# Four later modulation rounds of a two-block network: loaded over ScalarE's queue into the buffer of x and multiplied inside the first layer's attention

## The reference

```python
silu_c = jax.nn.silu(c)
silu_cc = jax.nn.silu(c_ctx)
for l in range(DEPTH):                               # DEPTH = 2
    mod = silu_c @ mod_w[l] + mod_b[l]
    mod_c = silu_cc @ mod_w[l] + mod_b[l]
    x, xc = trunk_layer(x, xc, mod, mod_c, ...)

# in trunk_layer
shift, scale, gate = jnp.split(mod[:, None, :], 3, axis=-1)
z = split_columns((rmsnorm(x, pre_g) * (1 + scale) + shift) @ w_in)
y_mla, yc_mla = mla_branch(...)                      # attention, 8 heads
y_pool = pool_branch(z, pool_w, pool_scale)
y_gla, yc_gla = gla_branch(...)                      # gated linear attention
out = merge_branches(z, y_mla, y_pool, y_gla, w_branch_mla, w_branch_pool, w_branch_gla, w_out)
x = x + gate * rmsnorm(out, post_g)
```

## Time and profile before

| what | value |
|---|---|
| median of 3 runs | 1536.61 us (1534.15 to 1538.3) |
| the profiled execution, its own time | 1537.87 us |
| its span in the profile | 1535.7 us |
| mean granted TensorE clock | 0.954 of full speed |
| PE busy | 1368.0 us, 89% of the span |
| ACT, DVE, POOL busy | 42%, 56%, 48% |
| DMA | 180.79 MB, 118 GB/s on average |

### The profile page before, as it was taken

How to read it: one execution, slowest core, us unless ns; L and a number is a source line. 1 busy time by engine, 2 the same in 40 slices (tenths; PEclk the granted TensorE clock), 3 DMA queues, 4 the chain that set the end, 5 groups by cost and what they waited for, 6 DMA issues and landing times.

```text
span 1535.7 us, 24492 instructions
## 1 busy us (share of the span) xinstructions
PE 1368.0 (89%) x10240; PEld 1147.7 (75%) x10240; DVE 864.3 (56%) x1237; ACT 638.4 (42%) x1004; POOL 733.3 (48%) x512
## 2 busy tenths in 40 slices
PE   5798899999999999688899899878799888799997
PEld 1654688777776788374888799868688777799996
DVE  2567514441423441756587468579898635588812
ACT  3545322433332324446334564747421123555542
POOL 0520054323223544050696658738644205499994
PEclk9899999999999999799999999979899999899998
DMA  8320033344334433030334335525222133355652
GB/s 333 130 69 14 29 96 96 110 153 163 112 133 181 137 97 98 27 122 15 123 122 133 104 124 153 164 83 178 70 85 70 56 97 118 90 188 181 183 186 86
DMA packets 49118, 180.79 MB, mean 118 GB/s; under 512 B 5488, under 2 KB 6512, under 8 KB 48624
## 3 DMA queue, kind: packets, MB, share of 16 engines
q1 hardware_dynamic: 48864, 177.13, 35.4%
q10 hardware_dynamic: 144, 2.10, 0.3%
HBM read 178.16 MB, written 1.05 MB: 117 GB/s over the span
## 4 chain that ended last, share of the span: by engine, by line
PE 67%; DVE 18%; ACT 5%; DMA 4%; issue 3%; POOL 2%; SPq 0%; ACTq 0%; DVEq 0%
PE ps L368 17%; PE ps L372 17%; PE ps L369 16%; PE ps L370 16%; DMA panels<-weights 3%; DVE work L1844 2%; POOL panels_r L412 1%; ACT panels_hi L402 1%; PE ps L965 1%; POOL panels_r L413 1%; DVE work L1286 1%; DMA const_sb<-constants 1%; DVE work_r L1289 1%; DVE small L1013 1%; DVE work L808 1%
## 5 line engine op out<-in xcount | busy, mean ns | idle before, releaser
L412 POOL TENSOR_TENSOR panels_r<-panels,panels_hi 128x512 fp32r<-128x512 f32 x254 | 373.0, 1468 | 782.2 <-ACT panels_hi L402 780.7
L369 PE MATMUL ps<-h_sb_r,panels_hi 128*128 128x256 f32 (+1 forms) x1408 | 452.9, 322 | 0.0
L402 ACT ACTIVATE panels_hi<-panels 128x1024 fp32r<-128x1024 f32 x254 | 267.6, 1057 | 407.9 <-PE ps L370 235.9
L413 POOL TENSOR_TENSOR panels_r<-panels,panels_hi 128x512 fp32r<-128x512 f32 x254 | 374.2, 1473 | 0.0
L368 PE MATMUL ps<-hi_sb_r,panels_hi 128*128 128x512 f32 (+1 forms) x784 | 278.1, 355 | 27.8 <-DVE h_sb_r L683 14.0
L369 PEld LDWEIGHTS ps<-h_sb_r,panels_hi 128*128 128x128 f32 x1408 | 276.0, 196 | 17.7 <-issue 0.7
L370 PE MATMUL ps<-hi_sb_r,panels_r 128*128 128x512 f32 (+1 forms) x784 | 272.1, 347 | 0.0
L368 PE MATMUL ps<-h_sb_r,panels_hi 128*128 128x256 f32 x624 | 184.1, 295 | 12.2 <-DVE h_sb_r L664 7.6
L368 PEld LDWEIGHTS ps<-hi_sb_r,panels_hi 128*128 128x128 f32 x784 | 152.4, 194 | 53.6 <-DVE h_sb_r L683 15.3
L368 PE MATMUL ps<-work_r,panels_hi 128*128 128x256 f32 (+1 forms) x560 | 177.0, 316 | 13.6 <-POOL panels_r L413 9.4
L370 PE MATMUL ps<-h_sb_r,panels_r 128*128 128x256 f32 x624 | 180.0, 288 | 0.0
(11 more groups left out here) (326 smaller groups left out, 1881.8 us busy)
## 6 DMA issues: line engine op xcount, KB each, us to landing
panels<-weights SPq DMA_DIRECT2D x328, 512.0 KB, 3.6
x_sb<-x_in SPq DMA_DIRECT2D x1, 2048.0 KB, 8.0
x_sb<-x_in ACTq DMA_DIRECT2D x1, 2048.0 KB, 10.7
const_sb<-constants SPq DMA_DIRECT2D x1, 1216.0 KB, 10.5
out<-x_sb SPq DMA_DIRECT2D x2, 512.0 KB, 3.1
vec_sb<-vectors SPq DMA_DIRECT2D x1, 725.0 KB, 11.8
small<-c_in SPq DMA_DIRECT2D x1, 8.0 KB, 1.8
```

What stands on the lines that cost most here:

```text
L369: pe.matmul(o, lhsT.hi, rhs.lo, start=False, stop=False)
L402: act.activation(panels_hi[:, m:m + PANEL * P], panels[:, n:n + PANEL * P], ACT.Copy).then_inc(panel_rounded, 1)
L412: pool.tensor_tensor(panels_r[:, at:at + half], panels[:, at:at + half], panels_hi[:, m:m + half], ALU.subtract)
L413: pool.tensor_tensor(panels_r[:, at + half:at + 2 * half], panels[:, at + half:at + 2 * half], panels_hi[:, m + half:m + 2 * half], ALU.su ...
```

## The change

The later rounds leave the merge and the ring. Their panels go to the end of the stream (`MOD_LATER`), SP no longer loads them, and ACT's queue loads them in 16 parts of 1 MB (two panels) into the two halves of `x_sb`. A part is a quarter of a round, 8 products. Part n is multiplied in step n+1 of the first layer's attention: parts 0, 4, 8 and 12 at the end of the step, the others between the scores and the transposes. The rounds are summed in bank 7, and so the values of attention, which used banks 6 and 7 in turn, use the two halves of bank 6 (in both layers, with a wait for `gated` that asks for one pair more).

```diff
+MOD_LATER = ((0, 2), (1, 0), (1, 1), (1, 2))
+MOD_PARTS = 4
+        lent_loaded, lent_used = [sem(f"mod_part_loaded{b}") for b in range(2)], sem("mod_part_used")
+        def load_mod_part(act, n):
+            if n >= 2:
+                act.wait_ge(lent_used, n - 1)
+            of = part_cols // (PANEL * P)
+            at = n_panels + of * n
+            act.dma_start(x_sb[:, n % 2 * part_cols:(n % 2 + 1) * part_cols].rearrange("p (n c) -> p n c", n=of),
+                          weights[at:at + of].rearrange("n p c -> p n c")).then_inc(lent_loaded[n % 2], 16)
+
+        def later_part(pe, n, bank):
+            r, a = divmod(n, MOD_PARTS)
+            i, ks = mod_index(*MOD_LATER[r]), KD // MOD_PARTS
+            if a == 0:
+                pe.wait_ge(mod_used, i)
+            pe.wait_ge(lent_loaded[n % 2], 16 * (n // 2 + 1))
+            for k in range(ks):
+                for j in range(MOD_GROUPS):
+                    c0 = n % 2 * part_cols + (k * MOD_GROUPS + j) * MOD_COLS
+                    mm = pe.matmul(ps[32 * j:32 * j + 32, bank, 0:MOD_COLS], silu_c[:, ks * a + k, :], x_sb[:, c0:c0 + MOD_COLS],
+                                   start=a == 0 and k == 0, stop=a == MOD_PARTS - 1 and k == ks - 1)
+            mm.then_inc(lent_used, 1)
@@ front_scalar
+                if l == 0:
+                    load_mod_part(act, 0)
+                    load_mod_part(act, 1)
@@ attn_tensor, behind the scores of item i
+                    if l == 0 and i - 1 in range(n_parts):
+                        if (i - 1) % MOD_PARTS:
+                            later_part(pe, i - 1, 7)
+                    if turned_round(i) is not None:
+                        mod_turn(pe, mod_index(*turned_round(i)), 7, MOD_COLS)
@@ attn_tensor, values
-                        if n >= 2:
-                            pe.wait_ge(gated, p0 + n - 1)
+                        if n >= 1:
+                            pe.wait_ge(gated, p0 + n)
@@ attn_tensor, end of step i
+                    if l == 0 and i - 1 in range(0, n_parts, MOD_PARTS):
+                        later_part(pe, i - 1, 7)
@@ attn_scalar, behind the copy of item i-2
+                    if l == 0 and i >= 2 and i in range(n_parts):
+                        load_mod_part(act, i)
+                    if l == 0 and i and i % MOD_PARTS == 0 and i <= n_parts:
+                        mod_copy(act, mod_index(*MOD_LATER[i // MOD_PARTS - 1]), 7)
@@ attn_vector, behind the scaling of item i-1
+                    if turned_round(i) is not None:
+                        l2, n = turned_round(i)
+                        mod_use(dve, mod_index(l2, n), l2, n, 7, MOD_COLS)
@@ items, gates, mixes of the merge: mod_half, mod_turn, mod_copy, mod_use go
-                    if l == 0 and i in MOD_HALVES:
-                        inputs.pool_banks_free(pe)
-                        l2, n, half = MOD_HALVES[i]
-                        mod_half(pe, mod_index(l2, n), l2, n, half, 3)
...
-                    if l == 0 and i in MOD_HALVES and MOD_HALVES[i][2] == 1:
-                        mod_turn(pe, mod_index(*MOD_HALVES[i][:2]), 3)
```

More of the change, by code:

```diff
@@ L178, in stream_plan @@
     add("ff_down", tiles_of("ffn_w_down_2", 0, FF, 0, D), split=True)
+    for l, n in MOD_LATER:
+        add_round(l, n, 0)
+        add_round(l, n, 1)
     return plan, order, split_panels
@@ L251, in build @@
         n_const += a.shape[1]
-    n_panels = -(-len(order) // PANEL)
+    l, n = MOD_LATER[0]
+    n_panels = plan[f"mod{l}_{n}_0"] // PANEL
     WORK = 25128
@@ L545, in mod_copy, with mod_use @@
             act.activation(row_sb, ps[:, bank, 0:MOD_COLS], ACT.Copy).then_inc(mod_row, 1)
-        def mod_use(dve, i, l, n, bank):
+        def mod_use(dve, i, l, n, bank, c0=0):
             step = steps["dve"]
@@ L937, in trunk, with turned_round @@
             scale = float(QK) ** -0.5
+            n_parts = MOD_PARTS * len(MOD_LATER)
+            def turned_round(i):
+                r, a = divmod(i - 1, MOD_PARTS)
+                return MOD_LATER[r - 1] if l == 0 and a == 0 and r - 1 in range(len(MOD_LATER)) else None
             def attn_tensor(pe):
@@ L1037, in attn_vector @@
                         dve.wait_ge(valued, p0 + n + 1)
-                        dve.tensor_tensor(y, ps[:, 6 + n % 2, 0:256], y, ALU.mult).then_inc(gated, 1)
+                        dve.tensor_tensor(y, ps[:, 6, n % 2 * 256:n % 2 * 256 + 256], y, ALU.mult).then_inc(gated, 1)
             attention = Stage(attn_tensor, attn_scalar, attn_vector, None)
@@ L1260, in items @@
                                        filled if k == 3 else None)
-                    if l == 0 and i in MOD_HALVES and MOD_HALVES[i][2] == 1:
-                        mod_turn(pe, mod_index(*MOD_HALVES[i][:2]), 3)
             def gates(act, first, end):
                 for i in range(first, end):
-                    if l == 0 and i in MOD_HALVES and MOD_HALVES[i][2] == 1:
-                        mod_copy(act, mod_index(*MOD_HALVES[i][:2]), 3)
                     rounding.before(act, "gate", l, i)
@@ L1291, in mixes @@
                                           ALU.subtract).then_inc(merged_ready[0], 1)
-                    if l == 0 and i in MOD_HALVES and MOD_HALVES[i][2] == 1:
-                        l2, n, _ = MOD_HALVES[i]
-                        mod_use(dve, mod_index(l2, n), l2, n, 3)
             def round_y(act, b):
@@ L1743, in second_half @@
         def second_half(prior, h_ready):
-            u_filled, u_taken = sem("u5_filled"), sem("u5_taken")
+            u_taken = sem("u5_taken")
+            u_filled, uf0 = shared("tile_filled", 4)
             bu_filled, bu_act, bu_dve = sem("bu_filled"), sem("bu_act"), sem("bu_dve")
```

25 lines of the change are left out of this document (14 added, 11 removed).

## The result

The changed kernel takes 1567.08 us (median of 4 runs, 1564.43 to 1570.14). The kernel before, timed beside it, takes 1537.23 us. The ratio is 1.0204, with a 95% interval from 1.0182 to 1.0226: slower by 2%. The profiled execution has a span of 1565.1 us, against 1535.7 before, and a granted clock of 0.94, against 0.954.

What follows compares the result with a forecast made beforehand. PE bounds the merge; first-layer attention is a chain from PE over DVE and ACT back. 1537.87 - 27.2 (merge) + 54.4 (attention) + 0.3 (last turn) + 17 (clock) = 1582.4 us, 1581 for the median; range 1556 to 1600.

Steps and rivals of the forecast that it cites:

- What the merge gives back: First layer's merge: PE loses 16 us of half rounds, 1.2 of turns and 10.0 of POOL waits; -27.2 us.
- The bound of -20: Merge: the smallest gain allowed for, in a span given as between -20 and -27.2 us.
- The order of the load: Attention: load n+1 is issued only when load n has landed and part n and the transposes are done; no overlap.
- Length of a load: Attention: a 1 MB load takes 5.1 us, from a line through 512 KB and 2 MB loads; ends 4.0 and 5.4.
- The steps, one by one: Attention: serial loads, counted step by step at full clock, make it 54.4 us longer.
- the cycle of 29.9 us: Attention: four items take two steps of 8.0 us, one of 7.3 and 6.6 from load 8 to load 9.
- over 105 us instead of some 53: Sign in the changed profile: length of attention, from first scores to the first full group of projections behind it.
- The clock: Attention: PE's gaps bring the lower clock; 26 us if always, two thirds taken, +17 us; granted clock 0.6 to 0.8.
- the rival with hidden loads: Attention: double buffering hides the loads, which grows by 9.1 us only; 1518 us at the median; chance 0.06.
- Serial loads, but the clock holds: Attention: loads in series, but the 17 us for the lower clock fall away; 1564 us; chance 0.2.

Runs made afterwards that it cites:

- the early issue: Changed kernel with ACT issuing part i's load at the head of step i, ahead of the exponential, not behind the copy of item i-2; 1526.66 us, ratio 0.9937.
- eight parts filled: Changed kernel with 16 more matmuls that add zeros ahead of the load's wait in eight parts, none in a round's first or second part; 1551.41 us, ratio 1.0108.
- the second profile: Profile of the changed kernel run once more, unaltered; 1566.92 us (6 runs), ratio 1.0197.
- A part of double length: Kernel with the early issue, eight more matmuls that add zeros in front of each of the twelve parts not first of a round; 1535.34 us, ratio 0.9991.
- the first part moved: Kernel with the early issue, each round's first part moved into the next step, its buffer's load issued behind the exponential; 1531.49 us, ratio 0.9986.

## Why the prediction was right, and where its sizes were off

The direction and the mechanism were right, and the time lay in the range; the number was 14 us too high. In the profiled execution 1582.4 us was forecast and 1567.0 came, 15.4 us less. The terms account for it: attention 19.2 us less, merge 1.7 less, and 5.8 more in two places where nothing was forecast. (That leaves 15.1; the 0.3 lie outside the spans.) The 5.8 us were luck for the number: without them it would have been 21 us too high.

**What the merge gives back**, forecast -27.2, measured -28.9 in the profile of the changed kernel and -32.3 with the rounds left out. PE's busy time fell by 17.4 us (16 and 1.2 were forecast) and its idle time by 11.5 (10.0 forecast). The bound of -20 was needless: nothing came in place of the waits for POOL, and the 3 us behind DVE stayed as they were.

**The order of the load.** Right, and shown from both sides: moving the issue on ACT frees it, and so, in part, does moving the part on PE. The issue lies behind a wait for the transposes, these lie behind the part, and that one waits for its own load. In every fourth step, where the part stands behind the transposes, it is the exponential's wait for DVE's maximum that holds the issue.

**Length of a load**: 5.1 us taken, 4.9 measured; half of it took 3.5. The Trainium skill's fit ("DMA: Bandwidth & Descriptors", section "Anatomy of one DMA") is made for GpSimd's path and gives an estimate of 4.4 us for this load and 3.2 for half of it. Here, on ACT's queue, the trace doesn't agree; both loads took 0.3 to 0.5 us more, and the line through rows of this case was nearer.

**The steps, one by one**: this is the term that was mis-sized. It stood at 54.4 us at the full clock. Measured, attention's +52.5 us split into 22.0 us more of idle time and 30.5 more of busy time. Of the busy time 16.5 are the new records at a high clock (with the early issue the same 530 take 69.27 us, 52.76 before), and 14.0 are slow rows. So at a high clock it would have been 38.5, not 54.4. The step that failed is the cycle of 29.9 us, with its 8.0 us from issue to issue and 6.6 from load 8 to load 9. I had put ACT's copy (0.6 us) and, in every fourth step, the exponential and the copy (1.34 and 0.38) ahead of the issue. The issue waits for neither. Load 5 went out at the start of the exponential, so part 5 had no wait for it at all (nor had part 13), where the forecast had one. With eight parts filled, where part and transposes run at the full clock, the step is 7.0 to 7.2 us instead of 8.0 and from load 8 to load 9 it is 5.4 instead of 6.6. The cycles that did come were 27.8 us from load 4 to load 8 and 30.2 from there to load 12 (149.77, 177.52, 207.71), near the forecast 29.9, but with the slow rows in them: two errors that cancelled, by luck, in the row that one would look at first. The sign "over 105 us instead of some 53" also had a wrong base: between these landmarks the kernel before takes 60.38 us.

**The clock**: +17 us was forecast, with two thirds of the rows at the lower level and the granted clock of the stretch at 0.6 to 0.8. It was 0.85 and, in the second profile, 0.80; the slow rows were 14.0 and 18.5 us. The term was right in size, and the level of the granted clock was not. The run with eight filled parts shows these rows on the path, and that they come from PE's idle time ahead of them. But the length of one wait does not decide it: part 3 ran at the lower clock after 2.50 us, and part 7 at the full one after 3.20 us (146.75 and 175.81).

**The parts' own work.** In the rival with hidden loads I had set PE's 7.6 us of free time against it, and so 1518 us. With hidden loads the kernel takes 1527 us, and its idle time is 8.3 us, not zero. A part of double length makes attention longer by all of it: the free time lies in waits inside the chain from PE over DVE and ACT, behind which the part stands as well.

**The rivals.** Hidden loads did not happen, for the reason given against them; the two moved lines make them happen. The Trainium skill's advice to double-buffer ("Trainium Kernel Development and Optimization", Best Practices) was met in the memory and not in the order: two buffers overlap nothing while the next issue stands behind the use of the present one. With the issue moved, the same two buffers gave the overlap that the page promises. "Serial loads, but the clock holds" gave 1564 us, closer than the forecast's 1581, and for a wrong reason: the clock did fall.

**Not forecast**: the rest's +4.6 us, which is the clock's, not the instructions'. Attention's start at +1.2 us came again in the second profile (124.81), but the other kernels with the same instructions ahead of it start anywhere from 123.45 to 125.03. What makes the difference was not tried, nor were the loads on another queue than ACT's.

## What to carry to other kernels

Two buffers are not yet an overlap: write down, for each load, which waits its issue stands behind, follow that back over the engines, and see if it leads to the use of the other buffer. If so, move the issue to the first place where its own buffer is free; here two lines turned +2% into -0.6%. When an engine gets waits of some us in every step, count its rows at the lower clock as well, on the path, and before taking credit for an engine's free time in a chain of dependent steps, see whether the new work would stand inside that free time or behind it.

## What the hardware showed that was not expected

- In these runs a DMA issue on ACT's queue did not wait for the ACT instructions ahead of it to run, but it was held by the waits that stand ahead of it. It went out at the start of the copy ahead of it (141.78 and 141.79), at the start of the exponential with the copy still to come (155.18 and 155.19), and 0.8 us before the copy in front of it (156.20 and 157.02), 0.09 us after the wait of the exponential had ended.
- How much two loads of 1 MB slow each other depended on how close together they were issued. One at a time they took 4.9 us (median). With the early issue, most 3 to 5 us apart, they took 4.7 to 5.7 us, median 5.0. Where two went out 1.5 to 1.8 us apart (the run with the first part moved), the second took 6.2 to 7.1 us. Once, with eight parts filled, a load with no other near it took 6.7 us as well, so this is seen and not explained.
- Executions of one and the same kernel differ by 10 us with the mean granted clock, 1560.6 us at 0.945 and 1570.3 us at 0.937, so a difference of a few us between two profiles must first be looked for in the length of equal records.
